# A product of experts with the tokens standing still: 512 moving columns instead of 288, and the sample rows apart in column groups

## The chip, the cores and the metric

The kernel runs on one NeuronCore of a Trainium2 chip, as one launch. The core has five engines that run their own instruction streams and meet only at semaphores: TensorE (PE, matrix products), VectorE (DVE), ScalarE (ACT), GpSimd (POOL) and SyncE (SP, here the queue that issues most transfers). The metric is device time in microseconds; 1143.01 is the median of three runs of the kernel before.

## The reference, cut to what matters

One layer of a decoder: a projection, a pooling mixer, a sparse attention, an output projection, and then a retrieval over 128 x 128 one-neuron experts (PEER). There are 256 prompt tokens and 32 sample tokens, 288 in all, of width 1024. Only the last part and its residual are touched:

```python
def trunk_layer(x, ...):
    ...
    x = x + jnp.concatenate([ya, yb], axis=-1) @ w_o
    x = x + peer(rms_norm(x, norm2_g), w_pq, sub_keys, expert_u, expert_v)

def peer(h, w_pq, sub_keys, expert_u, expert_v):
    ...
    # per token: top 16 of each of two lists of 128 keys, top 16 of their 256 sums, 8 heads:
    # eidx (N, 128) expert numbers, g (N, 128) softmax weights
    def body(args):
        xt, et, gt = args
        a = jax.nn.gelu(jnp.einsum('td,ted->te', xt, expert_u[et]), approximate=False)
        return jnp.einsum('te,ted->td', gt * a, expert_v[et])
```

The prompt rows and the sample rows are separate outputs. In the setup N_EXPERTS is 16384, D_MODEL 1024, PEER_HEADS 8.

## The kernel before, in words

The retrieval is computed densely. The experts are cut into NU = 128 blocks of 128 experts. In the **U stage** block n's inner products with all 288 tokens are made (`prod_u`), gelu is applied, and they are multiplied with the gate, which is zero for experts that a token did not choose. The result lies in `store`, 128 experts on the partitions, blocks by tokens along the row. In the **V stage** (`prod_v`) block v's gated activations are multiplied with its 128 x 1024 piece of expert_v and summed over all 128 blocks in PSUM.

Both products are made in the format fp32r with a correction: an operand is split into a high part and the rest (`w_hi`, `w_lo` of the weights, `h_hi`, `h_lo` of the tokens, `ag_hi`, `ag_lo` of the gated activations), and three terms are summed, high by high, high by low, low by high. ScalarE makes the high parts (`split_w`, `high_ag`; both through the helper `copy`, line 962), GpSimd subtracts to get `w_lo` (`low_w`, line 1340), VectorE subtracts to get `ag_lo` (`low_ag`, line 1655). SyncE loads each block's 512 KB into a ring of four (`w_raw`), and a slot is loaded again when PE has done the block (`prod_done`).

In the V stage before, the weights stand still: for each of eight chunks c of 128 output features there are three matmuls with the weights as the stationary operand (128 x 128) and all 288 tokens moving, into one PSUM bank for each chunk. The output is transposed, features on the partitions, and so is the residual `x_res`.

What comes ahead of it: VectorE selects the sample tokens' 256 best keys out of 1028 by rounds of `max` and `match_replace` on `work_s`, and line 1486 turns the result into a mask; PE spreads it (`sample_spread`, line 754) and goes on with the routing's query product (`rq`, line 729, and `rs`, line 744), the sample softmax follows (`pnew_ready` marks its two halves), then the sample's output projection (line 791), which uses four groups of 32 array columns side by side (`tile_position=(0, 32 * j)`), and the first weights of the U stage. During blocks 0 to 12 of the U stage PE also makes the sample tokens' query products (`rq_s`, line 849, in column groups too), and VectorE does the routing's top-16 selection until it has the slots, for which PE waits ahead of block 36 (transposes, line 477). From block 44 on the gates are spread (line 889) in 72 steps.

Each engine's order is the order in which its function below issues; nothing is reordered by a planner. `FRONT` is the number of U blocks that are written out, the others are loops. `tr` is the transpose on PE, line 477. The profile gives a matmul's line, and for fp32 operands it has two records for one matmul of the code.

## Time and profile before

| | us |
|---|---|
| median of three runs | 1143.01 (1140.9 to 1143.41) |
| the profiled execution | 1139.06 |
| its span, first to last instruction | 1136.9 |
| mean granted TensorE clock | 0.995 |
| PE busy / share | 1113.7 / 98% |
| GpSimd busy / share | 706.6 / 62% |
| VectorE busy / share | 616.2 / 54% |
| ScalarE busy / share | 430.9 / 38% |

A matmul's busy time is counted until its last result has left the array, and matmuls overlap, so a PE that is busy all the time says little about its pace. For that one reads the distance from one start to the next in a timeline.

### The profile page before, as it was taken

What the parts mean: (1) busy time and instruction counts of PE and PEld (TensorE: products, weight loads), DVE (VectorE), ACT (ScalarE), POOL (GpSimd) and SP (SyncE); (2) the same over time, 40 slices, a digit from 0 to 9 for tenths busy, and PEclk for the clock granted to TensorE, in tenths of its full rate; (3) what the DMA queues carried; (4) which work ended last, traced back from release to release, by engine and by line L of the source; (5) the groups of instructions that cost most, each with busy time, mean ns of one, the idle gap of its engine ahead of it and who ended that gap; (6) DMA issues with size and microseconds to landing.
All of it is one profiled execution on the core that took longest, in us unless ns stands there. A gap on an engine that the chain in (4) does not pass through costs nothing.

```text
span 1136.9 us, 24346 instructions
## 1 busy us (share of the span) xinstructions
PE 1113.7 (98%) x8263; PEld 1045.3 (92%) x8263; DVE 616.2 (54%) x1327; ACT 430.9 (38%) x750; POOL 706.6 (62%) x406
## 2 busy tenths in 40 slices
PE   7999998999999999999999999999999999999998
PEld 3448887899999999999999999999999999999998
DVE  2659999299998166666666671332222322222332
ACT  2133231343454433333333334444444444444442
POOL 4643434065776755555555557777777777777775
PEclk9999999999999999999999999999999999999999
DMA  9444577177654544444444445445555545444554
GB/s 334 121 115 130 169 260 265 66 274 256 206 160 137 167 130 129 126 128 126 127 127 128 128 128 160 154 166 166 166 166 166 165 162 165 161 166 161 164 166 174
DMA packets 64503, 186.62 MB, mean 164 GB/s; under 512 B 9157, under 2 KB 21069, under 8 KB 64068
## 3 DMA queue, kind: packets, MB, share of 16 engines
q1 hardware_dynamic: 59356, 178.60, 48.6%
q0 software_dynamic: 3824, 6.97, 2.0%
q10 hardware_dynamic: 1280, 0.53, 0.2%
q8 instruction: 22, 0.36, 0.1%
q14 instruction: 21, 0.17, 0.0%
HBM read 183.23 MB, written 3.00 MB: 164 GB/s over the span
## 4 chain that ended last, share of the span: by engine, by line
PE 78%; DVE 20%; DMA 1%; ACT 1%; issue 1%; DVEq 0%; SPq 0%
PE psum L944 36%; PE psum L878 25%; PE psum L889 6%; PE psum L493 4%; DVE top L1411 3%; DVE work_s L1412 2%; DVE rwork L1529 1%; DVE cand L1547 1%; PE psum L702 1%; PE psum L729 1%; DVE hit L1576 1%; DVE picked L1579 1%; DVE slots L1582 1%; DVE si L1535 1%; DVE si L1528 1%; PE psum L509 1%
## 5 line engine op out<-in xcount | busy, mean ns | idle before, releaser
L1340 POOL TENSOR_TENSOR w_lo<-w_raw,w_hi 128x1024 fp32r<-128x1024 f32 x256 | 614.5, 2402 | 316.3 <-ACT w_hi L962 316.3
L962 ACT ACTIVATE w_hi<-w_raw 128x1024 fp32r<-128x1024 f32 x256 | 271.7, 1061 | 238.4 <-DMA w_raw<-expert_v 224.7
L878 PE MATMUL psum<-h_hi,w_hi 128*128 128x288 f32 x1024 | 310.1, 303 | 0.0
L944 PE MATMUL psum<-ag_hi,w_hi 128*128 128x288 f32 x1024 | 301.4, 294 | 1.3 <-DVE ag_lo L1655 1.3
L878 PE MATMUL psum<-h_lo,w_hi 128*128 128x288 f32 x1024 | 302.6, 295 | 0.0
L878 PE MATMUL psum<-h_hi,w_lo 128*128 128x288 f32 x1024 | 302.1, 295 | 0.0
L944 PE MATMUL psum<-ag_hi,w_lo 128*128 128x288 f32 x1024 | 301.8, 295 | 0.0
L944 PE MATMUL psum<-ag_lo,w_hi 128*128 128x288 f32 x1024 | 301.5, 294 | 0.0
L1655 DVE TENSOR_TENSOR ag_lo<-store,ag_hi 128x288 fp32r<-128x288 f32 x128 | 121.1, 946 | 284.1 <-PE psum L944 282.9
L878 PEld LDWEIGHTS psum<-h_hi,w_hi 128*128 128x128 f32 x1024 | 192.8, 188 | 1.6 <-issue 1.6
L944 PEld LDWEIGHTS psum<-ag_hi,w_hi 128*128 128x128 f32 x1024 | 192.0, 188 | 1.5 <-issue 1.5
L878 PEld LDWEIGHTS psum<-h_hi,w_lo 128*128 128x128 f32 x1024 | 193.2, 189 | 0.0
L878 PEld LDWEIGHTS psum<-h_lo,w_hi 128*128 128x128 f32 x1024 | 193.1, 189 | 0.0
L944 PEld LDWEIGHTS psum<-ag_hi,w_lo 128*128 128x128 f32 x1024 | 192.1, 188 | 0.0
L944 PEld LDWEIGHTS psum<-ag_lo,w_hi 128*128 128x128 f32 x1024 | 192.0, 188 | 0.0
L1183 ACT ACTIVATE psum<-psum 128x288 f32<-128x288 f32 (+36 forms) x84 | 24.7, 294 | 211.3 <-PE psum L878 211.3
L1634 DVE COPY store<-psum 128x336 f32<-128x336 f32 (+35 forms) x72 | 25.9, 360 | 121.3 <-PE psum L889 121.3
L889 PE MATMUL psum<-i_hot,j_hot 128*128 128x128 f32 x576 | 75.8, 275 | 0.0
L889 PEld LDWEIGHTS psum<-i_hot,j_hot 128*128 128x128 f32 x576 | 71.4, 191 | 0.0
L340 POOL DMA_DIRECT2D v_cache<-cache_v x64 | 34.2, 534 | 56.9 <-issue 52.1
L729 PE MATMUL psum<-h,w_slice 128*128 128x256 f32 x256 | 60.1, 388 | 0.1
L729 PEld LDWEIGHTS psum<-h,w_slice 128*128 128x128 f32 x256 | 48.2, 194 | 7.5 <-issue 1.4
(261 smaller groups left out, 1058.4 us busy)
## 6 DMA issues: line engine op xcount, KB each, us to landing
w_raw<-expert_ut SPq DMA_DIRECT2D x128, 512.0 KB, 3.6
w_raw<-expert_v SPq DMA_DIRECT2D x128, 512.0 KB, 3.3
w_slice<-w_pq_cols SPq DMA_DIRECT2D x32, 512.0 KB, 5.6
w_most<-w_in_blocks SPq DMA_DIRECT2D x8, 699.0 KB, 12.8
w_slice<-w_o_half SPq DMA_DIRECT2D x8, 512.0 KB, 4.2
v_cache<-cache_v POOLq DMA_DIRECT2D x64, 64.0 KB, 3.3
w_o_sb<-w_o_half SPq DMA_DIRECT2D x8, 512.0 KB, 8.0
kT<-cache_kt SPq DMA_DIRECT2D x44, 64.0 KB, 2.0
```

The costliest lines, as they stand in the source:

```text
L340: eng.dma_start(dst[:, bass.ds((4 * i + (first + u)) * width, width)], cache[0, bass.ds(pg[u], 1), :, :].rearrange("a p d -> (a p) d")).th ...
L493: return pe.matmul(psum[:, 4 + (i + 1) % 4, 0:ZQ], hT[:, k, t * P:(t + 1) * P], w_cols(j, k), start=(k == 0), stop=(k == KC - 1))
L729: mm = pe.matmul(psum[:, r % 2, 0:SEQ], w_slice[:, (KC + r) % SLICES, k, :], h2[:, k, 0:SEQ], start=(k == 0), stop=(k == KC - 1))
L878: mm = pe.matmul(psum[:, 2 + s, 0:NT], a[:, s, c, :], b[:, c, :], start=(i == 0), stop=(i == 3 * KC - 1))
L889: mm = pe.matmul(psum[:, 6 + s % 2, b * NU:(b + 1) * NU], j_hot[:, s % 2, b, :], i_hot[:, s % 2, b, :], start=True, stop=True, skip_group_ ...
L944: mm = pe.matmul(psum[:, (c + 6) % 8, 0:NT], a[:, s, c, :], b, start=(first and i == 0), stop=(last and i == 2), skip_group_check=True)
L962: return act.activation(out, in_, ACT.Copy)
L1183: a = act.activation(psum[:, 2 + s, 0:done], psum[:, 2 + s, 0:done], ACT.Gelu)
L1340: pool.tensor_tensor(w_lo[:, s], w_raw[:, s], w_hi[:, s].bitcast(F32), ALU.subtract).then_inc(S["w_lo_ready"], 1)
L1411: settle(dve.max(best, left))
L1634: dve.tensor_copy(part[:, n:NU], g[:, n:NU])
L1655: dve.tensor_tensor(ag_lo[:, s % 2, :], store[:, bass.ds(v, 1)].rearrange("p a t -> p (a t)"), ag_hi[:, s, :].bitcast(F32), ALU.subtract). ...
```

## The change

Five things are changed.

1. In the V stage the operands change places. The gated activations of 128 prompt tokens are stationary, and 512 columns of expert_v move. There are four outputs of 128 tokens x 512 features (`Y_ORDER`), three terms each: 12 matmuls for a block. First come the eight with `w_hi`, then, behind the wait for `w_lo_ready`, the four with `w_lo_v`.
2. The 32 sample tokens are kept out of that. Their gated activations (`ag_s`, copied by VectorE) are stationary in plain fp32, and `w_raw` moves: four matmuls of 256 columns, one in each group of 32 array columns, ahead of the twelve.
3. The residual is kept by token. During U blocks 13, 15, 17, 19 and 21 PE transposes x1 (`x1_rows`), ScalarE copies it to `x_rows`, and SP saves it at block 23 instead of saving `xT` at block 11. `FRONT` goes from 16 to 24 for that. The final addition and the output are by rows.
4. GpSimd's low part of the weights goes to a buffer of two (`w_lo_v`) in the V stage, where it was a ring of four; it waits for `prod_done`.
5. GpSimd's `h_lo` of the prompt tokens waits for `pnew_ready`, 2 as well.

```diff
-    ag_hi = at("ag_hi", cur[0], [P, RING, NT], F32R)
-    ag_lo = at("ag_lo", cur[0] + RING * NT, [P, 2, NT], F32R)
+    ag_hi = at("ag_hi", cur[0], [P, RING, SEQ], F32R)
+    ag_lo = at("ag_lo", cur[0] + RING * SEQ, [P, 2, SEQ], F32R)
+    ag_s = at("ag_s", cur[0] + (RING + 2) * SEQ, [P, 2, NS])
...
+    w_lo_v = at("w_lo_v", cur[0], [P, 2, KC, P], F32R)
...
-    FRONT = 16
+    FRONT = 24
+    X_ROWS_AT = (13, 15, 17, 19, 21)
+    Y_ORDER = ((0, 0), (0, 1), (1, 0), (1, 1))
...
+            def x1_rows(i):
+
+                if i >= 2:
+                    pe.wait_ge(S["x_rows_copied"], i - 1)
+                for q in range(4):
+                    if i < 4:
+                        mm = tr(psum[:, 6 + i % 2, q * P:(q + 1) * P], xT[:, 4 * (i % 2) + q, (i // 2) * P:(i // 2 + 1) * P])
+                        continue
+                    for a in range(2):
+                        mm = pe.matmul(psum[32 * q:32 * q + 32, 6, a * P:(a + 1) * P], xT[:, 2 * q + a, SEQ:NT],
+                                       ident[:, :], start=True, stop=True, tile_position=(0, 32 * q),
+                                       skip_group_check=True)
+                mm.then_inc(S["x_rows_psum"], 1)
...
             def prod_v(s, v, first=False, last=False):
 
                 pe.wait_ge(S["w_hi_ready"], v + (NU + 1))
-                pe.wait_ge(S["w_lo_ready"], v + (NU + 1))
                 pe.wait_ge(S["ag_hi_ready"], v + 1)
                 pe.wait_ge(S["ag_lo_ready"], v + 1)
-                for c in range(KC):
-                    if first and c == 0:
-                        pe.wait_ge(S["g_done"], G_STEPS)
-                    if first and c >= 4:
-                        pe.wait_ge(S["act_free"], NU + (c - 7))
-                    i = 0
-                    for a, b in ((w_hi, ag_hi[:, s, :]), (w_hi, ag_lo[:, s % 2, :]), (w_lo, ag_hi[:, s, :])):
-                        mm = pe.matmul(psum[:, (c + 6) % 8, 0:NT], a[:, s, c, :], b, start=(first and i == 0), stop=(last and i == 2), skip_group_check=True)
-                        i += 1
+                if first:
+                    pe.wait_ge(S["g_done"], G_STEPS)
+                    pe.wait_ge(S["act_free"], NU - 3)
+                for j in range(4):
+                    mm = pe.matmul(psum[32 * j:32 * j + 32, 2, 0:2 * P], ag_s[:, s % 2, :],
+                                   w_raw[:, s, 2 * j:2 * j + 2, :].rearrange("p c d -> p (c d)"), start=first,
+                                   stop=last, tile_position=(0, 32 * j), skip_group_check=True)
+                if last:
+                    mm.then_inc(S["y_psum"], 1)
+                def v_term(i, a, b, start=False, stop=False):
+
+                    t, h = Y_ORDER[i]
+                    return pe.matmul(psum[:, (i + 6) % 8, :], a[:, t * P:(t + 1) * P],
+                                     b[:, 4 * h:4 * h + 4, :].rearrange("p c d -> p (c d)"), start=start, stop=stop,
+                                     skip_group_check=True)
+
+                for i in range(4):
+                    v_term(i, ag_hi[:, s, :], w_hi[:, s], start=first)
+                    v_term(i, ag_lo[:, s % 2, :], w_hi[:, s])
+                pe.wait_ge(S["w_lo_ready"], v + (NU + 1))
+                for i in range(4):
+                    mm = v_term(i, ag_hi[:, s, :], w_lo_v[:, s % 2], stop=last)
                     if last:
                         mm.then_inc(S["y_psum"], 1)
...
             pool.wait_ge(S["h_hi_p"], 1)
+            pool.wait_ge(S["pnew_ready"], 2)
             pool.tensor_tensor(h_lo[:, :, 0:SEQ], h2[:, :, 0:SEQ], h_hi[:, :, 0:SEQ].bitcast(F32), ALU.subtract
                                ).then_inc(S["h_lo_p"], 1)
...
-            with pool.Fori(1, LAST // RING) as m:
+            with pool.Fori(1, NU // RING) as m:
                 for s in range(RING):
                     low_w(s, RING * m + s)
+
+            def low_v(s, v, done):
+                pool.wait_ge(S["w_hi_ready"], v + (NU + 1))
+                pool.wait_ge(S["prod_done"], done)
+                pool.tensor_tensor(w_lo_v[:, s % 2], w_raw[:, s], w_hi[:, s].bitcast(F32), ALU.subtract
+                                   ).then_inc(S["w_lo_ready"], 1)
+
+            for s in range(RING):
+                low_v(s, s, NU + max(s - 1, 0))
+            with pool.Fori(1, NU // RING) as m:
+                for s in range(RING):
+                    low_v(s, RING * m + s, RING * m + (NU + s - 1))
...
-                dve.tensor_tensor(ag_lo[:, s % 2, :],
-                                  store[:, bass.ds(v, 1)].rearrange("p a t -> p (a t)"),
-                                  ag_hi[:, s, :].bitcast(F32), ALU.subtract).then_inc(S["ag_lo_ready"], 1)
+                row = store[:, bass.ds(v, 1)].rearrange("p a t -> p (a t)")
+                dve.tensor_copy(ag_s[:, s % 2, :], row[:, SEQ:NT])
+                dve.tensor_tensor(ag_lo[:, s % 2, :], row[:, 0:SEQ], ag_hi[:, s, :].bitcast(F32), ALU.subtract
+                                  ).then_inc(S["ag_lo_ready"], 1)
...
-            for c in range(KC):
-                dve.wait_ge(S["y_psum"], c + 1)
-                dve.tensor_tensor(x_res[:, c, :], x_res[:, c, :], psum[:, (c + 6) % 8, 0:NT], ALU.add
-                                  ).then_inc(S["y_added"], 1)
+            dve.wait_ge(S["x_res_in"], 32)
+            dve.wait_ge(S["y_psum"], 1)
+            dve.tensor_tensor(x_res_s[:, :], x_res_s[:, :], psum[:, 2, 0:2 * P], ALU.add).then_inc(S["y_added"], 1)
+            for i, (t, h) in enumerate(Y_ORDER):
+                dve.wait_ge(S["y_psum"], i + 2)
+                rows = x_res[:, t, BANK * h:BANK * (h + 1)]
+                dve.tensor_tensor(rows, rows, psum[:, (i + 6) % 8, :], ALU.add).then_inc(S["y_added"], 1)
```

On PE, one block inside the V stage's loop stood so before; the last three rows go on in the same pattern up to 24 matmuls:

```order
L944 MATMUL psum<-ag_hi,w_hi 128x288 [waits ag_lo_ready,ag_hi_ready]
L944 MATMUL psum<-ag_lo,w_hi 128x288
L944 MATMUL psum<-ag_hi,w_lo 128x288
L944 MATMUL psum<-ag_hi,w_hi 128x288
L944 MATMUL psum<-ag_lo,w_hi 128x288
L944 MATMUL psum<-ag_hi,w_lo 128x288
```

And the same block on PE now, whole:

```order
L965 REGISTER_ALU [waits w_hi_ready]
L971 MATMUL psum<-w_raw,ag_s 32x256 [waits ag_lo_ready,ag_hi_ready]
L971 MATMUL psum<-w_raw,ag_s 32x256 x3
L979 MATMUL psum<-w_hi,ag_hi 128x512
L979 MATMUL psum<-w_hi,ag_lo 128x512
L979 MATMUL psum<-w_hi,ag_hi 128x512
L979 MATMUL psum<-w_hi,ag_lo 128x512
L979 MATMUL psum<-w_hi,ag_hi 128x512
L979 MATMUL psum<-w_hi,ag_lo 128x512
L979 MATMUL psum<-w_hi,ag_hi 128x512
L979 MATMUL psum<-w_hi,ag_lo 128x512
L979 MATMUL psum<-w_lo_v,ag_hi 128x512 [waits w_lo_ready]
```

Three more of the last row follow. The wait for the low weights has moved behind eight matmuls, and four matmuls on 32 array columns stand at the head of each block.

On GpSimd the U stage's and the V stage's subtractions were one loop, before:

```order
L1335 TENSOR_TENSOR h_lo<-h_90,h_hi 128x8x256 [waits h_hi_p]
L1340 TENSOR_TENSOR w_lo<-w_raw,w_hi 128x1024 [waits w_hi_ready]
L1345 TENSOR_TENSOR h_lo<-h_90,h_hi 128x8x32 [waits h_hi_s]
L1340 TENSOR_TENSOR w_lo<-w_raw,w_hi 128x1024 [waits w_hi_ready] x3
L1350 UNCONDITIONAL_BRANCH
```

Now, on GpSimd, the first of them has a further wait, and the V stage has rows of its own:

```order
L1387 TENSOR_TENSOR h_lo<-h_92,h_hi 128x8x256 [waits pnew_ready,h_hi_p]
L1392 TENSOR_TENSOR w_lo<-w_raw,w_hi 128x1024 [waits w_hi_ready]
L1397 TENSOR_TENSOR h_lo<-h_92,h_hi 128x8x32 [waits h_hi_s]
...
L1409 TENSOR_TENSOR w_lo_v<-w_raw,w_hi 128x1024 [waits prod_done,w_hi_ready] x4
L1414 UNCONDITIONAL_BRANCH
```

What moved: the first row now stands behind VectorE's sample softmax, and the V stage's subtractions behind PE's blocks.

## Rows read from the trace of the kernel before

**Rows 1.** The page: busy times, and the group of one line.

```profile
PE 1113.7 (98%) x8263; PEld 1045.3 (92%) x8263; DVE 616.2 (54%) x1327; ACT 430.9 (38%) x750; POOL 706.6 (62%) x406
...
L1340 POOL TENSOR_TENSOR w_lo<-w_raw,w_hi 128x1024 fp32r<-128x1024 f32 x256 | 614.5, 2402 | 316.3 <-ACT w_hi L962 316.3
```

**Rows 2.** The chain that ended last, by line, and its V part in time.

```profile
PE psum L944 36%; PE psum L878 25%; PE psum L889 6%; PE psum L493 4%; DVE top L1411 3%; DVE work_s L1412 2%; DVE rwork L1529 1%; DVE cand L1547 1%; PE psum L702 1%; PE psum L729 1%; DVE hit L1576 1%; DVE picked L1579 1%; DVE slots L1582 1%; DVE si L1535 1%; DVE si L1528 1%; PE psum L509 1%
...
725.34 404.50 PE psum L944 x3051
```

**Rows 3.** Busy time in a stretch of V: length, PE, PEld, DVE, ACT, POOL, clock, DMA.

```profile
900.00:1000.00 100.00, 100.00 (x757) 100.00 (x756) 28.99 (x32) 43.67 (x63) 75.47 (x32) 1.00 0.50 163
```

**Rows 4.** PE's timeline, 187 to 224 us: start, length, what.

```profile
187.79 0.61 PE L744 MATMUL psum<-keysT,q_ring 128*128 128x128 f32 x4
188.23 3.62 PE L729 MATMUL psum<-h,w_slice 128*128 128x256 f32 x16
191.69 0.61 PE L744 MATMUL psum<-keysT,q_ring 128*128 128x128 f32 x4
...
218.79 3.66 PE L791 MATMUL psum<-w_o_sb,catT 128*32 128x256 f32 x64
222.38 1.13 PE L729 MATMUL psum<-h,w_slice 128*128 128x256 f32 x4
223.34 0.38 PE L477 MATMUL psum<-ident,wo_rows 128*128 128x128 f32 x2
```

**Rows 5.** PE's timeline around the first L849 group.

```profile
238.43 0.29 PE L878 MATMUL psum<-h_hi,w_lo 128*128 128x288 f32 x1
238.65 1.95 PE L849 MATMUL psum<-w_slice,h 128*32 128x128 f32 x64
240.54 0.40 PE L878 MATMUL psum<-h_hi,w_hi 128*128 128x288 f32 x1
240.78 0.30 PE L878 MATMUL psum<-h_lo,w_hi 128*128 128x288 f32 x1
```

**Rows 6.** PE's timeline behind 363 us, and a stretch: length, busy, clock, DMA.

```profile
363.89 0.82 PE L477 MATMUL psum<-ident,slots 128*32 128x128 f32 x3 [2.29 <-DVE slots L1600]
364.75 0.44 PE L878 MATMUL psum<-h_lo,w_hi 128*128 128x288 f32 x1
364.99 0.44 PE L878 MATMUL psum<-h_hi,w_lo 128*128 128x288 f32 x1
...
364.40:368.00 3.60, 3.60 (x20) 0.63 0.00 0
```

**Rows 7.** Timelines of POOL, DVE and PE, 189 to 224 us, and one stretch.

```profile
189.76 4.53 POOL L1335 TENSOR_TENSOR h_lo<-h,h_hi 128x2048 fp32r<-128x2048 f32 x1
...
190.64 4.74 DVE L1486 TENSOR_TENSOR work_s<-work_s,score_s 32x1028 f32<-32x1028 f32 x1
197.17 1.22 DVE L1493 TENSOR_TENSOR log_s<-log_s,psum 128x1024 f32<-128x1024 f32 x1 [1.01 <-PE psum L754]
223.76 0.48 DVE L1510 TENSOR_TENSOR xT<-xT,psum 128x128 f32<-128x128 f32 x2 [15.39 <-PE psum L477]
...
196.22 0.91 PE L754 MATMUL psum<-bias_s,fold 32*128 32x512 bf16 x3 [3.93 <-DVE bias_s L1488]
197.06 5.06 PE L729 MATMUL psum<-h,w_slice 128*128 128x256 f32 x16
...
195.00:215.00 20.00, 18.78 (x208) 0.91 0.08 27
```

**Rows 8.** The start of V on PE; durations (min/median/max ns) of L1655.

```profile
725.34 0.37 PE L944 MATMUL psum<-ag_hi,w_hi 128*128 128x288 f32 x1 [1.30 <-DVE ag_lo L1655]
...
L1655 DVE TENSOR_TENSOR ag_lo<-store,ag_hi x128: 457/926/2424, 722.7 to 1126.4; 128x288 fp32r<-128x288 f32 x128
```

**Rows 9.** The end of V: DVE's additions, and PE's last matmul.

```profile
1129.93 3.18 DVE L1672 TENSOR_TENSOR x_res<-x_res,psum 128x288 f32<-128x288 f32 x8 [2.55 <-PE psum L944]
...
1132.33 0.29 PE L944 MATMUL psum<-ag_hi,w_lo 128*128 128x288 f32 x1
```

More of the change, by code:

```diff
@@ L289, in hybrid_kernel @@
     eq_ps = psum[:, 1, :].rearrange("p (b i) -> p b i", b=NB)
-    x1_save = nc.dram_tensor("x1_save", [P, KC, NT], F32, kind="Internal").ap()
+    x1_save = nc.dram_tensor("x1_save", [P, 2, D], F32, kind="Internal").ap()
+    x1_save_s = nc.dram_tensor("x1_save_s", [P, 2 * P], F32, kind="Internal").ap()
     S = Named(nc, ctx)
@@ L455, in _ @@
                         load_slice(q + i)
[L456 to L457 removed]
+                if n == FRONT - 1:
+                    sp.wait_ge(S["x_rows_copied"], len(X_ROWS_AT))
+                    sp.dma_start(x1_save, x_rows[:]).then_inc(S["x1_saved"], 16)
+                    sp.dma_start(x1_save_s, x_rows_s[:]).then_inc(S["x1_saved"], 16)
             with sp.Fori(FRONT // RING + 1, NU // RING) as m:
@@ L466, in _ @@
             sp.dma_start(x_res[:], x1_save).then_inc(S["x_res_in"], 16)
-            for c in range(0, KC, 2):
-                sp.wait_ge(S["y_added"], c + 2)
-                sp.dma_start(y_t[:, c:c + 2, :], x_res[:, c:c + 2, :]).then_inc(S["out_done"], 16)
-            sp.wait_ge(S["out_done"], 16 * (1 + KC // 2))
+            sp.dma_start(x_res_s[:], x1_save_s).then_inc(S["x_res_in"], 16)
+            sp.wait_ge(S["y_added"], 1)
+            sp.dma_start(y_rows_s, x_res_s[:]).then_inc(S["out_done"], 16)
+            for i, (t, h) in enumerate(Y_ORDER):
+                sp.wait_ge(S["y_added"], i + 2)
+                sp.dma_start(y_rows[:, t, BANK * h:BANK * (h + 1)], x_res[:, t, BANK * h:BANK * (h + 1)]
+                             ).then_inc(S["out_done"], 16)
+            sp.wait_ge(S["out_done"], 16 * (2 + len(Y_ORDER)))
         @block.tensor
@@ L904, in _ @@
                     rs_s(n // 3 - 1)
+                if n in X_ROWS_AT:
+                    x1_rows(X_ROWS_AT.index(n))
             with pe.Fori(FRONT // RING, SLOTS_AT // RING) as m:
@@ L1202, in _ @@
                     copy(q_tr[:, i % 2, :], psum[:, 7, 0:P]).then_inc(S["q_tr_copied"], 1)
+                if n in X_ROWS_AT:
+                    i = X_ROWS_AT.index(n)
+                    act.wait_ge(S["x_rows_psum"], i + 1)
+                    if i < 4:
+                        a = copy(x_rows[:, i // 2, BANK * (i % 2):BANK * (i % 2 + 1)], psum[:, 6 + i % 2, :])
+                    else:
+                        a = copy(x_rows_s[:, :], psum[:, 6, 0:2 * P])
+                    a.then_inc(S["x_rows_copied"], 1)
                 if n == 13:
@@ L1241, in high_ag @@
                     act.wait_ge(S["prod_done"], v + (NU - 3))
-                copy(ag_hi[:, s, :], store[:, bass.ds(v, 1)].rearrange("p a t -> p (a t)")
+                copy(ag_hi[:, s, :], store[:, bass.ds(v, 1)].rearrange("p a t -> p (a t)")[:, 0:SEQ]
                      ).then_inc(S["ag_hi_ready"], 1)
@@ L1728 @@
     r = run_bass_kernel_spmd(nc, [a], core_ids=[0])
-    y = np.ascontiguousarray(r.results[0]["y_t"].transpose(2, 1, 0)).reshape(SEQ + DB * DS, D)
-    return (y[:SEQ].reshape(1, SEQ, D), y[SEQ:].reshape(DB, DS, D)) + tuple(r.results[0][n] for n, _ in outs[1:])
+    y = np.ascontiguousarray(r.results[0]["y_rows"].transpose(1, 0, 2)).reshape(1, SEQ, D)
+    y_s = np.ascontiguousarray(r.results[0]["y_rows_s"].reshape(4, DB * DS, 2 * P).transpose(1, 0, 2))
+    return (y, y_s.reshape(DB, DS, D)) + tuple(r.results[0][n] for n, _ in outs[2:])
```

16 lines of the change are left out of this document (9 added, 7 removed).

## The prediction

> **What bounds the kernel now.** I read the page first, then the chain that ended last, the busy time by stretches, PE's timeline at the places where it changes its kind of work, and the waits. On the page TensorE (PE) is busy for 98% of the span, GpSimd (POOL) for 62%, VectorE (DVE) for 54% [rows 1]; but busy PE is not PE at its peak, so the chain is the better witness: 25% of it is one line of PE, L878, the U stage, and 36% is another, L944, the V stage [rows 2]. In that stage nothing stops PE: from 725.34 us the chain has 3051 matmul records in 404.50 us, 132.6 ns each, without a wait [rows 2], so a block of 24 matmuls takes 24 x 132.6 = 3.182 us. GpSimd works 75.5 us in 100 us there, VectorE 29 and ScalarE 44 [rows 3]. The V stage therefore costs what PE's instruction stream costs, and that is where this change has to be priced. Ahead of the U stage, up to 232 us, the chain runs through VectorE's selection and short PE pieces, and a microsecond saved there counts in full.
>
> **The V stage, per block.** The change takes 24 matmuls of 288 columns away and puts in 12 of 512 columns (four outputs, three terms) and four fp32 matmuls of 256 columns, one for each group of 32 array columns.
>
> The four small ones have an exact likeness: L791 issues the same shape, fp32, stationary 32 tokens, 256 columns, j innermost. It gave 64 records for 32 matmuls, so an fp32 matmul is two records. A plain fp32 stretch of 256 columns has 16 records in 191.69 - 188.23 = 3.46 us, a step of 0.216 [rows 4]. L791's 64 records go in 16 steps of four, so the four groups do run side by side: 16 x 0.216 = 3.456. Two steps a block: 0.432 us. But L791 lasts 222.38 - 218.79 = 3.59 us, 0.13 more than its steps, and the four L729 records behind it take 0.96 (to 223.34) against 4 x 0.216 = 0.864, 0.10 more [rows 4]. The whole trip, out of fp32r matmuls and back into them, stands at L849, inside the U stage: 0.22 from the last 288-column matmul where 0.133 is usual, 1.89 for 16 steps that take 0.110 elsewhere (187.79 to 188.23 for four), 0.24 to the second matmul behind it: 0.09 + 0.13 + 0.11 = 0.33 [rows 4, 5]. I take 0.334. Before, that trip was made in a few places; now it is made in each of 128 blocks.
>
> The Trainium skill weighs in here from both sides. "TensorEngine Tiling (Array Packing)", Key Properties, says that changing the tiling mode drains the engine; it has no price for it. "TensorE: Matmul & The Clock Gate", Measured speedup vs the span model, has a group of column tiles last one matmul plus about 4 ns for each further tile, and no charge around it; by that the sample part would be the 0.432 alone and the block 0.33 us shorter than I sum it.
>
> The 12 wide ones have no likeness: no fp32r matmul here has another width than 288. Bare streaming of 288 columns is 0.120 us at 2.4 GHz (at 1.2 GHz, granted clock 0.5 to 0.63, the step is 0.24, 364.75 to 364.99 [rows 6]); the full-clock step is 0.1326, so 12.6 ns come on top. The fp32 steps have only some 3 ns on top (0.216 for two passes of 256 columns). Three readings for 512 columns: the 12.6 are paid once per matmul, 213.3 + 12.6 = 226; they grow with the columns, 132.6 x 512/288 = 236; or they vanish when a matmul is long, as with fp32, 216. I take 226, the middle one: the one row there is says 12.6 per matmul, and nothing in it says per column. 216 and 236 are the bounds.
>
> Block: 12 x 0.226 + 0.432 + 0.334 = 3.478 us (3.358 with 216, 3.598 with 236), against 3.182. Over 128 blocks: **+37.9 us** (+22.5, +53.2). Even with free overheads per matmul the trip of 0.33 outweighs what longer matmuls give back: 24 x 12.6 = 0.30 us was all the excess there was.
>
> What else moves there is covered. GpSimd's subtraction (2.40 us [rows 1]) now waits until the block two before is done, but PE asks for it only behind eight wide matmuls, about 2.6 us into the block; GpSimd has a block and a half. ScalarE copies 256 instead of 288 columns, 44% busy. The DMA per block is the same 512 KB in a longer period.
>
> **The front.** The row part of h_lo (POOL L1335, 4.53 us) moves behind the sample softmax. Before, it ran from 189.76 to 194.29, and VectorE's L1486, 1028 elements of 32 rows, took 4.74 us beside it; a two-source operation of 128x1024 takes 1.22 alone (L1493) [rows 7]. VectorE lost 3.5 us, and PE stood 3.93 us for its result. After that wait PE ran at a lower pace: the 16 records of L729 behind it took 5.06 instead of 3.62, 1.44 more, with the granted clock at 0.91 over the stretch 195 to 215 [rows 4, 7], and the L754 group ahead of them shares in it; I count 1.6 that a wait of 0.4 would not cost. In the new place GpSimd has VectorE's idle time: VectorE stands 15.39 us before L1510 [rows 7]. Everything up to the first product hangs on this chain: **-5.1 us** (-3.5 if the slow stretch stays).
>
> **The U stage.** New on PE: 16 transposes and a group of eight small fp32 matmuls. No transpose stands in the rows; I price one at the step of a 128-column record, 0.11 [rows 4], 16 x 0.11 = 1.8. The last group (eight matmuls, 16 records) has 16 steps of 0.11 if pairs on one column group run one behind the other and 4 if all run side by side, plus one trip: 0.8 to 2.1, I take 1.3. Together 3.1. Against that stands PE's only wait of the U stage, 2.29 us at 363.89 for the routing's slots, with a slow stretch behind it: 20 matmul records in 3.6 us at clock 0.63 where 27 fit, and half-pace pieces before, some 1.2 us [rows 6]. PE now comes 3.1 us later to a result that doesn't move, so both go: 3.1 - 2.3 - 1.2 = **-0.4 us** (-0.9 to +0.4). The five copies lie in idle time of ScalarE (38% busy over the span [rows 1]); the save to memory is as large as before and waits at a place where only later loads are queued behind it on SP, with three blocks already loaded.
>
> **Start and end of V.** Before, PE waited 1.30 us at 725.34 for VectorE's ag_lo, which then took 2.42 us, its longest, where its median is 0.93 [rows 8], GpSimd's subtractions running beside it. GpSimd now starts on V only when the last product is done, and PE needs fewer of the gates: 1.3 us go. But GpSimd then runs two subtractions on end while VectorE wants ag_lo for the second block; I give 0.5 back: **-0.8 us** (-1.5 to +0.7). At the end VectorE added each output while PE made the next: eight in 3.18 us, the last 0.78 us behind the last matmul's start [rows 9]. Now the four wide ones stop within 0.7 us, and four additions of 512 columns, 0.6 us each (between 0.40 for 288 and 1.22 for 1024 [rows 7, 9]), end 2.2 us behind it: **+1.4 us**. The output's transfer is of about the same size.
>
> **Sum.** -5.1 - 0.4 - 0.8 + 37.9 + 1.4 = +33.0. On the profiled execution (span 1136.9, with what lies around it 1139.06) that makes 1172.1. The median of the runs is 1143.01, 3.95 above that execution; the time asked for is compared with such medians, so I add the change to it: **1176.0 us**.
>
> **Rivals.**
> - *The excess per matmul vanishes with width* (step 216): 1176.0 - 15.4 = 1160.6. For it: the fp32 steps of 128 and of 256 columns carry 3 ns at most, whatever their length. Against it: their loads come at most once in 107 ns of streaming too (0.110 for 128 columns), and there the excess is as small, so a load alone doesn't make it; something of fp32r does. Chance 0.17. The Trainium skill, "TensorE: Matmul & The Clock Gate", Back-to-back issue gap, gives this as its rule (columns / 2.4 + 2.5 ns when warm); for 288 columns it would say 122.5 where the trace has 132.6, so here it is off for fp32r.
> - *It grows with the columns* (236): 1176.0 + 15.3 = 1191.3. For it: at half clock there is no excess at all, as if full speed outran the operand's supply. Against it: nothing in the trace. Chance 0.28.
> - *The trip is not paid in the loop* (small matmuls slip in beside the wide ones). Block 12 x 0.226 + 0.432 = 3.144, -4.9 us over 128, in all 1143.0 - 5.1 - 0.4 - 0.8 - 4.9 + 1.4 = 1133.2, faster. It decides from a trip below 0.08 us on (0.20 with 216). Against it: both places that are read above, 0.33 each. For it: those were single trips in other surroundings. Chance 0.06.
> - *VectorE becomes the bound.* Its copy and subtraction for block v wake with GpSimd's subtraction, both by the end of block v-2. Between the two, GpSimd can step in: 0.2 + 2.40 + 0.42 and some 0.1 of signals make 3.1 us; there are 3.48 less about 0.25, 3.2. With GpSimd at 2.5 or more it binds, and each 0.1 us costs 12.8. ag_lo went up to 2424 ns in this stage [rows 8]. At 0.1 us: 1189. Chance 0.07.
> - Forecast: 0.42.
>
> **How the numbers follow.** Forecast and the two neighbours of the step and VectorE's case hold 0.94 of the chance; the range goes from 1158 (216, less 2.6 for the small terms) to 1193 (236, plus 1.7). Faster by over 0.2% only in the third rival, 0.06; within 0.2% (2.3 us, about what a measurement here can tell) 0.02; slower 0.92.
>
> **What would show it.** In the V stage of the changed kernel: a period of 3.48 us from one block's first small matmul to the next; steps of 0.226 between wide matmuls; about 0.33 us at the seams, where the first wide matmul's record is longer than its fellows. L1486's heir at 1.2 us with PE waiting under 1 us, and no 2.3 us wait before the slots' transposes. It would be wrong if the seams were invisible, if PE waited for ag_lo each block, or if the wide step were outside 216 to 236.

## The result and the profile after

The change makes the kernel slower: 1177.09 us in the median of 4 runs (1175.0 to 1177.97) against 1142.23 us (1140.9 to 1143.41) for the kernel before on the same chip, a ratio of 1.0303 [1.0283, 1.0323]. The prediction was 1176.0 us, in a range from 1158 to 1193. The profiled execution of the changed kernel took 1177.8 us, with a span of 1176.1.

The page's first part again, and from its fifth part VectorE's costliest group (line, engine, operation, out<-in, count | busy us, mean ns of one | idle time before it and what ended it), to set against [rows 1]:

```profile
PE 1157.4 (98%) x7783; PEld 938.0 (80%) x7783; DVE 833.0 (71%) x1452; ACT 428.5 (36%) x755; POOL 707.5 (60%) x406
...
L1720 DVE COPY ag_s<-store 128x32 f32 (+1 forms) x128 | 300.3, 2346 | 104.8 <-PE psum L979 103.1
```

TensorE is 98% busy as before, with fewer and longer matmuls. VectorE is up from 54% to 71%, and one line makes it: a copy of 32 columns, 2346 ns on average.

The stretch that answers to [rows 3] (length, busy time of PE, PEld, DVE, ACT and POOL, then clock, DMA share, GB/s):

```profile
900.00:1000.00 100.00, 100.00 (x573) 66.39 (x566) 77.83 (x57) 39.48 (x58) 68.67 (x29) 1.00 0.46 148
```

PE is busy without a gap; GpSimd has 29 subtractions in it instead of 32: fewer blocks come through in the same time.

PE's timeline in V, one whole block from seam to seam (start, length to the end of the last, line, what, how many):

```profile
899.62 0.64 PE L971 MATMUL psum<-w_raw,ag_s 128*32 128x256 f32 x8
900.19 0.50 PE L979 MATMUL psum<-w_hi,ag_hi 128*128 128x512 f32 x1
900.53 0.39 PE L979 MATMUL psum<-w_hi,ag_lo 128*128 128x512 f32 x1
...
902.14 1.07 PE L979 MATMUL psum<-w_lo_v,ag_hi 128*128 128x512 f32 x4
903.14 0.64 PE L971 MATMUL psum<-w_raw,ag_s 128*32 128x256 f32 x8
```

The period is 903.14 - 899.62 = 3.52 us; 124 of the stage's 127 periods have it. Read it by starts. From the second wide matmul (900.53) to the ninth (902.14) are seven steps in 1.61 us, 0.230 each; of the four of w_lo_v the 1.07 us less one record's 0.39 are three steps, 0.227. Over the block the wide step is 0.2294. What is left of 3.520 after 12 x 0.2294 = 2.753 and two small steps of 0.216 is the trip, the loss at going from the wide matmuls into the column groups and back: 0.335 us. It shows where it was expected: the first wide matmul behind the small ones is 0.50 long instead of 0.39, and the next starts 0.34 behind it (900.19 to 900.53) instead of 0.23.

The front and the borders of the stages, on PE, VectorE and GpSimd, against [rows 6 to 9]:

```profile
192.30 1.22 DVE L1550 TENSOR_TENSOR work_s<-work_s,score_s 32x1028 f32<-32x1028 f32 x1
194.36 0.60 PE L768 MATMUL psum<-bias_s,fold 32*128 32x512 bf16 x3 [0.42 <-DVE bias_s L1552]
194.89 3.72 PE L743 MATMUL psum<-h,w_slice 128*128 128x256 f32 x16
205.02 4.54 POOL L1387 TENSOR_TENSOR h_lo<-h,h_hi 128x2048 fp32r<-128x2048 f32 x1 [14.93 <-DVE pnew L1568]
228.58 0.38 PE L892 MATMUL psum<-h_hi,w_hi 128*128 128x288 f32 x1
...
360.97 0.50 PE L491 MATMUL psum<-ident,slots 128*32 128x128 f32 x3 [0.35 <-DVE slots L1664]
...
719.56 0.29 PE L892 MATMUL psum<-h_hi,w_lo 128*128 128x288 f32 x1
719.78 0.64 PE L971 MATMUL psum<-w_raw,ag_s 128*32 128x256 f32 x8
...
1170.09 2.48 DVE L1740 TENSOR_TENSOR x_res<-x_res,psum 128x512 f32<-128x512 f32 x4 [1.75 <-PE psum L979]
```

VectorE's operation takes 1.22 us instead of 4.74, PE waits 0.42 us instead of 3.93, and the 16 records behind the wait take 3.72 us instead of 5.06. The waits of 2.29 and 1.30 us at the slots and at the start of V have become 0.35 and none. Yet the first product (228.58) is only 3.5 us earlier than before (232.08), and VectorE's operation starts 1.7 us later than its forerunner did (190.64). From the start of that operation to the first product it is 36.28 us against 41.44, 5.2 us less; the rest was lost ahead of it. A row of before and the windows of the two executions say where (before first, then after; the last three figures are clock, DMA share, GB/s):

```profile
232.08 0.38 PE L878 MATMUL psum<-h_hi,w_hi 128*128 128x288 f32 x1
...
110.00:148.00 38.00, 36.15 (x205) 30.30 (x207) 35.54 (x49) 9.36 (x21) 14.96 (x28) 1.00 0.61 192
```

```profile
110.00:148.00 38.00, 36.13 (x181) 31.21 (x183) 33.92 (x48) 9.37 (x21) 15.04 (x28) 0.96 0.59 179
```

In this execution of the changed kernel TensorE had a stretch at the lower clock level between 110 and 148 us, in code that the change doesn't touch. Of the eight kernels below that keep its front, none has it there. In six of them the first product stands at 226.5 to 227.0 us, 5.1 us or more earlier than before; the other two come as late as the changed kernel, with a granted clock of 0.94 over their first 60 us.

### The profile page after: what moved, and what is told of

The parts are those of the page before. It is cut to its first block, busy times and chain, and to the rows that moved or that the text cites. A ratio compares the mean times of both kernels' runs of the same rounds, so it can differ in the third digit from the quotient of the medians.

```text
span 1176.1 us, 23563 instructions
## 1 busy us (share of the span) xinstructions
PE 1157.4 (98%) x7783; PEld 938.0 (80%) x7783; DVE 833.0 (71%) x1452; ACT 428.5 (36%) x755; POOL 707.5 (60%) x406
## 4 chain that ended last, share of the span: by engine, by line
PE 87%; DVE 9%; DMA 2%; SPq 1%; issue 1%; ACT 0%; DVEq 0%; ACTq 0%
PE psum L892 33%; PE psum L979 32%; PE psum L971 6%; PE psum L903 5%; PE psum L507 3%; DVE top L1475 2%; DVE work_s L1476 2%; DMA w_rest<-w_in_blocks 2%; PE psum L743 2%; PE psum L716 1%; PE psum L491 1%; PE psum L686 1%; PE psum L863 1%; SPq L374 1%; DVE work_p L1476 1%; DVE picked L1643 1%
## 5 line engine op out<-in xcount | busy, mean ns | idle before, releaser
L1392 POOL TENSOR_TENSOR w_lo<-w_raw,w_hi 128x1024 fp32r<-128x1024 f32 x128 | 307.4, 2404 | 195.6 <-ACT w_hi L1005 195.5
L1409 POOL TENSOR_TENSOR w_lo_v<-w_raw,w_hi 128x1024 fp32r<-128x1024 f32 x128 | 308.1, 2408 | 143.6 <-PE psum L979 138.2
L1720 DVE COPY ag_s<-store 128x32 f32 (+1 forms) x128 | 300.3, 2346 | 104.8 <-PE psum L979 103.1
L979 PE MATMUL psum<-w_hi,ag_hi 128*128 128x512 f32 x512 | 214.3, 419 | 0.0
L979 PE MATMUL psum<-w_hi,ag_lo 128*128 128x512 f32 x512 | 201.5, 394 | 0.0
L979 PEld LDWEIGHTS psum<-w_hi,ag_hi 128*128 128x128 f32 x512 | 96.0, 187 | 69.0 <-issue 52.7
L979 PE MATMUL psum<-w_lo_v,ag_hi 128*128 128x512 f32 x512 | 136.8, 389 | 0.0
L979 PEld LDWEIGHTS psum<-w_lo_v,ag_hi 128*128 128x128 f32 x512 | 96.1, 188 | 20.9 <-POOL w_lo_v L1409 0.4
L979 PEld LDWEIGHTS psum<-w_hi,ag_lo 128*128 128x128 f32 x512 | 96.4, 188 | 17.2
L971 PE MATMUL psum<-w_raw,ag_s 128*32 128x256 f32 x1024 | 81.8, 391 | 0.0
```

The source lines that it names most:

```text
L971: mm = pe.matmul(psum[32 * j:32 * j + 32, 2, 0:2 * P], ag_s[:, s % 2, :], w_raw[:, s, 2 * j:2 * j + 2, :].rearrange("p c d -> p (c d)"), s ...
L979: return pe.matmul(psum[:, (i + 6) % 8, :], a[:, t * P:(t + 1) * P], b[:, 4 * h:4 * h + 4, :].rearrange("p c d -> p (c d)"), start=start, ...
L1392: pool.tensor_tensor(w_lo[:, s], w_raw[:, s], w_hi[:, s].bitcast(F32), ALU.subtract).then_inc(S["w_lo_ready"], 1)
L1409: pool.tensor_tensor(w_lo_v[:, s % 2], w_raw[:, s], w_hi[:, s].bitcast(F32), ALU.subtract).then_inc(S["w_lo_ready"], 1)
L1720: dve.tensor_copy(ag_s[:, s % 2, :], row[:, SEQ:NT])
```

## The experiments

Each kernel is the changed kernel with one edit, but for the one with the copy out of the way, which builds on the one ahead of it, and the last, which is the kernel before with one edit. "Before" in each comparison ran on the same chip. Distances to the changed kernel are distances between separate series of runs, on three chips or more: the kernel before has medians from 1140.12 to 1142.23 us in these series, so up to 2 us of such a distance can be the chip's or that of the executions taken.

**Late h_lo taken back.** GpSimd no longer waits before the row part of h_lo:

```diff
-            pool.wait_ge(S["pnew_ready"], 2)
             pool.tensor_tensor(h_lo[:, :, 0:SEQ], h2[:, :, 0:SEQ], h_hi[:, :, 0:SEQ].bitcast(F32), ALU.subtract
```

> The changed kernel with GpSimd's row part of h_lo back where it was, ahead of the sample softmax. Theory: VectorE's comparison of 1028 elements again takes 4.7 us instead of 1.2, PE waits 3.9 us for it and runs on at the lower clock for a while: 5.2 us more than the changed kernel, about 1182. Rival: only VectorE's 3.5 us come back and the slower stretch of PE was chance: about 1180.5. Second rival: the wait moved is worth nothing because the v_cache pages or the softmax are late anyway: 1177.

Measured: 1182.43 us (1182.05 to 1182.82), ratio 1.0368 [1.0341, 1.0394], 5.3 us above the changed kernel. Its VectorE, GpSimd and PE:

```profile
190.37 4.74 DVE L1549 TENSOR_TENSOR work_s<-work_s,score_s 32x1028 f32<-32x1028 f32 x1
...
189.50 4.52 POOL L1386 TENSOR_TENSOR h_lo<-h,h_hi 128x2048 fp32r<-128x2048 f32 x1
...
195.96 1.03 PE L768 MATMUL psum<-bias_s,fold 32*128 32x512 bf16 x3 [3.94 <-DVE bias_s L1551]
196.92 6.33 PE L743 MATMUL psum<-h,w_slice 128*128 128x256 f32 x15
```

The whole of the old picture is back: VectorE's operation at 4.74 us beside GpSimd's, the wait of 3.94 us, and slow matmuls behind it. From the start of VectorE's operation to the first product (233.43) it is 43.06 us, where the changed kernel has 36.28. The front's gain is this one wait.

**Wide matmuls cut in two.** Each 512-column matmul becomes two of 256; same stationary operand, twice the instructions:

```diff
-                    return pe.matmul(psum[:, (i + 6) % 8, :], a[:, t * P:(t + 1) * P],
+                    for k in range(2):
+                        mm = pe.matmul(psum[:, (i + 6) % 8, 2 * P * k:2 * P * (k + 1)], a[:, t * P:(t + 1) * P],
```

> The changed kernel with each of the 12 wide matmuls cut into two of 256 columns, same operands. It measures what a full-width fp32r matmul costs beside its columns (0.2294 us for 512 columns, 0.1326 for 288). If the extra is fixed per matmul (13 to 16 ns): step 0.120 to 0.123, block 3.65 to 3.71 us, 17 to 24 us more, 1194 to 1201. If it grows with the columns: step 0.115, block 3.52, 1177. If a stationary load with what goes with it takes 0.132 whatever the width (288 columns would then have been bound by the load): step 0.132, block 3.94, 54 us more, about 1231.

Measured: 1190.62 us (1189.79 to 1191.92), ratio 1.0442 [1.0414, 1.047]; the period is 3.63 us. That is nearest to the first case, and a little below its ranges (3.65 to 3.71, 1194 to 1201). Its timeline:

```profile
900.43 0.40 PE L980 MATMUL psum<-w_hi,ag_lo 128*128 128x256 f32 x2
900.67 0.40 PE L980 MATMUL psum<-w_hi,ag_hi 128*128 128x256 f32 x2
```

Two matmuls of 256 columns take 0.24 us (0.120 each by the records' starts), 13 ns above bare streaming (106.7). For 288 columns it was 12.6 above 120, for 512 it is 13 to 16 above 213.3. So the excess is nearly one price per matmul: neither proportional to the columns (that would give 0.118 x 2 = 0.236 for 512, where 0.2294 was measured) nor absent in long ones. At 256 columns "per matmul" and "per column" lie close (0.119 and 0.118); it is 256, 288 and 512 together that tell them apart.

**Order of the terms.** Four matmuls with ag_hi, then four with ag_lo, instead of in turn:

```diff
                 for i in range(4):
                     v_term(i, ag_hi[:, s, :], w_hi[:, s], start=first)
+                for i in range(4):
                     v_term(i, ag_lo[:, s % 2, :], w_hi[:, s])
```

> The changed kernel with the eight matmuls on w_hi in another order: four with ag_hi, then four with ag_lo, where they alternated. In the changed kernel the eight steps on w_hi are 0.228 to 0.236 us and the four on w_lo_v 0.227. If alternating stationary operands are what costs the difference: all steps 0.227, 2 to 4 us less, 1173 to 1175. If it is the moving operand's place in memory or other engines' traffic: no difference, 1177.

Measured: 1177.14 us (1175.86 to 1179.04), ratio 1.0323 [1.0293, 1.0352], and a period of 3.52 us. The order is worth nothing.

**The trip once for two blocks, first attempt.** The small matmuls of an even block wait and run with those of the odd one; the even block's w_raw is held a block longer for them:

```diff
-                    sp.wait_ge(S["prod_done"], RING * m + (NU + s - RING + 1))
+                    sp.wait_ge(S["prod_done"], RING * m + (NU + s - RING + 1 + (s + 1) % 2))
...
+                if s % 2:
+                    pe.wait_ge(S["ag_s_ready"], v + 1)
+                    for b in (s - 1, s):
+                        for j in range(4):
```

> The changed kernel with the small matmuls of two blocks made together at the head of every second block, the same matmuls in number and kind. Theory (the trip into the column groups and back costs 0.335 us each time): 64 trips fewer, a pair of blocks takes 6.705 instead of 7.040 us, 21.4 us less, about 1155.5. Rival (the loss lies in the small matmuls' own columns or in the wide steps, whatever surrounds them): 1177. Second rival (VectorE's chain of copy and subtraction binds once the blocks are unequal): between, 1160 to 1170, with PE waiting for ag_lo or ag_s.

Measured: 1202.64 us (1200.42 to 1203.64), ratio 1.054 [1.051, 1.057]; missed by 47 us, to the wrong side. The costliest of its waits from 800 to 1000 us (who waits for whom: us in total, times, longest):

```profile
ACT w_hi L1009 <- DMA w_raw<-expert_v: 129.7, 29, 8.9
```

Two heads of pairs on PE:

```profile
877.36 1.07 PE L972 MATMUL psum<-w_raw,ag_s 128*32 128x256 f32 x16
...
884.07 1.07 PE L972 MATMUL psum<-w_raw,ag_s 128*32 128x256 f32 x16
```

ScalarE waits up to 8.9 us for the weights: holding a slot of the ring of four longer sends two loads off together and late, and everything behind them is late. The edit carried a second change, and that one decided the time. The trace still says something on the trip: where the loads are in time, a pair of blocks takes 884.07 - 877.36 = 6.71 us, the 6.705 that the theory has for one trip in two blocks.

**The trip once for two blocks, one block early.** Ahead of an even block's wide matmuls stand its own small ones and the next block's, so that every slot is released as before; VectorE copies the sample columns of both blocks at once, ahead of the even block's ag_lo:

```diff
+                if s % 2 == 0:
+                    pe.wait_ge(S["w_hi_ready"], v + (NU + 2))
+                    for b in (s, s + 1):
+                        for j in range(4):
...
+                if s % 2 == 0:
+                    dve.tensor_copy(ag_s[:, s:s + 2, :],
+                                    store[:, bass.ds(v, 2)][:, :, SEQ:NT])
```

> The small matmuls of two blocks stand together again, this time one block early: ahead of the even block's wide matmuls those of this block and of the next one, so no slot of the weight ring is held longer than in the changed kernel. If the 0.335 us that each block loses goes at the change between the small column-group matmuls and the wide ones (theory), two blocks lose it once: 2 x (12 x 0.2294 + 0.432) + 0.335 = 6.705 us instead of 7.040, 64 x 0.335 = 21.4 us less than the changed kernel, 1155.7 us, between 1153 and 1158. If the time is lost anew at each group of four small matmuls, whatever stands ahead of it (rival), 1177 us as now. If the copy of the samples' activations, two blocks' at once, comes late behind GpSimd's subtraction (second rival), waits on it appear in the chain and the time lies in between.

Measured: 1182.41 us (1181.47 to 1184.14), ratio 1.0374 [1.0353, 1.0395]; a miss, in the direction of the second rival and beyond it. One turn of the chain:

```profile
903.94 3.36 DMA w_raw<-expert_v
...
908.37 0.41 ACT ag_hi L1009
...
908.85 1.83 issue
910.68 0.42 DVE ag_lo L1727
...
911.33 1.07 PE psum L974 x16
```

The 1.83 us that the chain calls issue is the copy: VectorE's timeline has it from 908.32 for 2.44 us, with GpSimd's subtraction beginning at 908.31. A weight block is now wanted one block earlier, and load, ScalarE's two operations, the copy and ag_lo make a loop that takes longer than PE's work.

**The same, with the copy out of the way.** The copy for the next two blocks is made behind the odd block's ag_lo:

```diff
+                if s % 2 and not last:
+                    copy_ag_s((s + 1) % RING, v + 1)
```

> The pair of blocks again, with VectorE's copy of the samples' activations taken out of the way: it is made for the next two blocks after the odd block's ag_lo, instead of ahead of the even block's. In the pair kernel before this one VectorE's copy could start only 2.4 us before TensorE wanted ag_lo, and the block took 3.58 us on a loop over the weight load, the two engines' copies and TensorE. If that copy was what closed the loop (theory), TensorE bounds again and the trip is paid once for two blocks: 1155.7 us, between 1153 and 1158. If the loop over the load is closed by something else, since a weight block is wanted one block earlier than in the changed kernel (rival), it stays at 1170 to 1182 us with waits on w_hi or ag_lo in the chain.

Measured: 1166.16 us (1165.24 to 1166.74), ratio 1.0223 [1.0197, 1.025]: 10.9 us below the changed kernel and 10.5 above what the theory gave, so outside its range and outside the rival's. The chain, nearly all PE now:

```profile
895.67 2.62 DVE ag_lo L1724
...
898.52 1.07 PE psum L974 x16
899.59 5.66 PE psum L983 x24
...
909.39 2.63 DVE ag_lo L1724
```

The heads of three pairs in PE's timeline:

```profile
898.52 1.07 PE L974 MATMUL psum<-w_raw,ag_s 128*32 128x256 f32 x16 [0.27 <-DVE ag_lo L1724]
...
905.18 1.07 PE L974 MATMUL psum<-w_raw,ag_s 128*32 128x256 f32 x16
...
912.24 0.64 PE L974 MATMUL psum<-w_raw,ag_s 128*32 128x256 f32 x8 [0.28 <-DVE ag_lo L1724]
```

From 898.52 to 905.18 two blocks go by in 6.66 us, with 16 small records and one trip, where two blocks of the changed kernel take 7.04; 6.705 had been worked out, with every wide step at 0.2294, and here those of the second block are 0.227. So the trip is paid for each change to the column groups, not for each group of four. The next pair takes 7.06, and so it goes on: 32 of 63 pairs take 6.66 to 6.71 us, the other 31 take 7.04 to 7.09. What is missing of the 21.4 us is mostly a new wait: every second time ag_lo itself (0.41 us alone) lasts 2.62 us beside GpSimd's subtraction, and PE stands for it (6.1 us in 22 times from 800 to 1100 us, so 0.28 each). That is once in four blocks, 9 us over 128.

**One column group of the four.** The loop over the groups ends after the first:

```diff
-                for j in range(4):
+                for j in range(1):
```

> Of the four small matmuls of a block only that of the first column group is left, so three quarters of the sample rows of y are left out. The four ran beside each other in 0.432 us. If the round trip is paid for going into any 32-column group (theory), the block stays at 12 x 0.2294 + 0.432 + 0.335 = 3.520 us and the time at 1177 us. If the trip is the wait for four groups to drain (rival), it shrinks towards a quarter of 0.335 us, and the time towards 1145 us. The fp32 matmul over all 128 columns took the place of the four at 0.06 us more than nothing for the trip, so this tells the group itself from the number of groups.

Measured: 1173.06 us (1172.87 to 1173.7), ratio 1.0288 [1.0262, 1.0314]. Its timeline:

```profile
903.24 0.62 PE L971 MATMUL psum<-w_raw,ag_s 128*32 128x256 f32 x2
903.78 0.50 PE L979 MATMUL psum<-w_hi,ag_hi 128*128 128x512 f32 x1
...
906.74 0.62 PE L971 MATMUL psum<-w_raw,ag_s 128*32 128x256 f32 x2
```

The period is 3.50 us: the other three groups cost 0.02 together, the trip stands as it was. The number of groups is not what it costs. The time is 4 us below the 1177 expected. Of the spans' distance 2.6 us are these 0.02 in each block, and 2.0 lie ahead of the first product (226.55 against 228.58).

**Full width in place of the groups.** One fp32 matmul with 128 stationary columns takes the place of the four:

```diff
-                for j in range(4):
-                    mm = pe.matmul(psum[32 * j:32 * j + 32, 2, 0:2 * P], ag_s[:, s % 2, :],
+                mm = pe.matmul(psum[:, 2, 0:2 * P], w_raw[:, s, 4, :],
```

> In each block one full-width fp32 matmul (128 stationary columns, 256 moving) takes the place of the four in 32-column groups; it multiplies a block of the weights with itself, so the sample rows of y are left out. By the theory that the round trip is the price of using column groups, it vanishes: 12 x 0.2294 + 0.432 = 3.185 us for a block instead of 3.520, 1177.1 - 128 x 0.335 = 1134.2 us. By the rival that it is the price of going from fp32r to fp32 operands and back, the block stays at 3.52 us and the time at 1177 us. If both share it, between them.

Measured: 1139.54 us (1138.92 to 1141.16), ratio 0.9994 [0.9983, 1.0005], 37.6 us below the changed kernel, between what the theory (1134.2) and the rival (1177) gave and near the theory. Its timeline:

```profile
900.11 0.63 PE L970 MATMUL psum<-w_raw 128*128 128x256 f32 x2
900.40 0.58 PE L978 MATMUL psum<-w_hi,ag_hi 128*128 128x512 f32 x1
...
903.34 0.61 PE L970 MATMUL psum<-w_raw 128*128 128x256 f32 x2
```

900.11 to 903.34 is a period of 3.23 us (3.24 on average over the stage). Less 12 wide steps (at 0.2294, as in the changed kernel) and two small ones, 0.05 is left of the trip. So going from fp32r to fp32 and back costs some 0.05 us, going into 32-column groups and back the other 0.28. The Trainium skill, "TensorEngine Tiling (Array Packing)", Key Properties, says that a change of the tiling mode drains the engine. This run and the one with a single group agree that the change costs something whatever the number of groups, and put its price at 0.28 us for the way in and back.

**No small matmuls** in any block but the first and the last:

```diff
-                for j in range(4):
+                for j in range(4 if first or last else 0):
```

> The small matmuls are left out of all blocks but the first and the last, so the sample rows of y miss most of their sum; everything else stays. By the theory the wide matmuls alone take 12 x 0.2294 = 2.753 us for a block; TensorE then no longer bounds the loop everywhere, since VectorE's pair (the copy of 2.35 us behind GpSimd's subtraction, and 0.41 us) and the waits between the engines take about 2.99 us for a block. So 1177.1 - 126 x 0.53 = 1110 us, with waits of TensorE on what VectorE hands over; if TensorE stays the bound (rival), 1177.1 - 126 x 0.767 = 1080 us; a wide step that needs more time than 0.2294 without the small ones between would show as a block over 2.753 us without a wait.

Measured: 1109.14 us (1107.76 to 1110.26), ratio 0.9725 [0.9706, 0.9744]. The number is that of the theory, its loop only in part. The chain through four blocks:

```profile
903.74 5.77 PE psum L979 x24
...
909.67 3.17 DMA w_raw<-expert_v
...
913.90 0.41 ACT ag_hi L1005
...
914.38 0.84 issue
915.22 0.42 DVE ag_lo L1721
...
915.78 0.47 PE psum L979
```

Two blocks of PE, then load, ScalarE, VectorE (the copy hides in the 0.84 called issue), and PE again: 915.78 - 903.74 = 12.04 us for four blocks, 3.01 each. VectorE is on the loop, but so is the load. The changed kernel has 14.08 us for the same four blocks, which is why none of this binds there.

**The kernel before with the late h_lo alone.** The one edit of the change that gained:

```diff
             pool.wait_ge(S["h_hi_p"], 1)
+            pool.wait_ge(S["pnew_ready"], 2)
```

> The kernel before with one edit of the change alone: GpSimd's subtraction that makes h_lo of the prompt tokens waits for the new pool rows, as in the changed kernel, so that it no longer stands in the way of VectorE there. By the theory the front's gain of the change is this wait and nothing else, and taking it back cost the changed kernel 5.3 us; so 1142.2 - 5.2 = 1137.0 us, faster than both kernels, between 1136 and 1138.5. By the rival that the gain of the front belongs to the new placing of buffers or of the program in memory, 1142 us.

Measured: 1135.43 us (1133.72 to 1135.93, 6 runs) against 1140.12 (17 runs), ratio 0.9955 [0.9939, 0.997]. It is 4.7 us faster than the kernel before, the fastest kernel of this study that computes everything, and 0.6 us below the range expected. Its profiled execution:

```profile
194.47 0.60 PE L754 MATMUL psum<-bias_s,fold 32*128 32x512 bf16 x3 [0.41 <-DVE bias_s L1489]
195.01 3.72 PE L729 MATMUL psum<-h,w_slice 128*128 128x256 f32 x16
...
360.49 0.50 PE L477 MATMUL psum<-ident,slots 128*32 128x128 f32 x3 [2.29 <-DVE slots L1601]
```

The front is as in the changed kernel, with 36.28 us from the start of VectorE's operation to the first product, and the wait of 2.29 us at the slots is still there.

## Why the prediction was right

Its terms were made against the profiled execution, so the spans are compared: 1176.1 - 1136.9 = +39.2 us, where the terms added up to +33.0.

- **The V stage**, forecast +37.9, measured from first to last matmul 1170.3 - 719.8 = 450.6 against 407.0: +43.6 us. The mechanism held in all its parts: a period without a wait, small matmuls in two steps of 0.216, a trip of 0.335 (0.334 forecast). That the trip belongs to the change into column groups, and is paid for each such change, was argued from two places; the pair of blocks at 6.66 us, the single group and the full-width matmul show it. The one mis-sized term is the wide step, 0.2294 instead of 0.226: 12 x 128 x 0.0034 = 5.2 us. Another 0.3 us lies in the stage's first two periods, 3.81 and 3.56 us: in the first, PE's first matmul on the low weights starts at 722.46, right behind the subtraction that GpSimd had begun at 720.00.
- **The readings of the wide step.** Of 216, 226 and 236 the middle one was nearest, and the 256-column kernel shows it as a price per matmul of some 13 ns; at 512 columns it is 14 on w_lo_v and mostly 18 to 20 on w_hi, 16 in the mean, so "per matmul" is the nearest of the three readings and not exact. The Trainium skill's rule of columns / 2.4 + 2.5 ns ("TensorE: Matmul & The Clock Gate", Back-to-back issue gap), which the page gives for the isolated gap of one matmul and which was the rival with 216, gives 109, 122.5 and 215.8 ns for 256, 288 and 512 columns where the traces have 120, 132.6 and 229: for fp32r the measurement decides against it. The price per matmul doesn't explain why the steps on w_hi take 0.231 and those on w_lo_v 0.227. The order of the terms isn't it, and in the kernel with paired blocks and the copy out of the way some blocks ran all 12 at 0.227. Which other engine's traffic or which sequence makes the 4 ns was not found.
- **The front**, forecast -5.1, in the profiled execution -3.5. The part on VectorE and PE came as forecast (PE's wait 0.42, full pace behind it), and 1.7 us were lost to a slow stretch elsewhere that comes and goes between executions. Counted from the start of VectorE's operation, behind that stretch, the front is 41.44 us before and 36.28 after, -5.16. The single-edit kernels give it as 5.3 us one way and 4.7 the other in the medians; their profiled executions had slow stretches of their own (0.97 and 0.94 over the first 60 us), and behind them 43.06 and 36.28 us.
- **The U stage**, forecast -0.4: from the first to the last product 490.98 us against 491.66, -0.7. PE's new work took the place of the wait for the slots, and the slow stretch behind that wait is gone.
- **The start of V**, forecast -0.8: 0.22 us from the last product to the first small matmul against 1.60, -1.4; the half microsecond set aside for the second block's ag_lo was not needed, since it was made by 722.78 and PE came to that block at 723.59.
- **The tail**, forecast +1.4: 1.2 us. VectorE's four additions take 2.48 us.
- **The step from span to median.** The prediction added the change to the median of the runs, on the ground that the profiled execution of before was 3.95 us below it. The medians moved by 34.9 us, the profiled executions by 38.7: that of before was a fast one of its kind, that of after was not. The forecast for the profiled execution was 1172.1, 5.7 us under the 1177.8 that it took; the 3.95 us added, and 0.7 by which the median of after lies below its profiled execution, took 4.7 of these back. That the total is 1.1 us off is luck to this extent. The base was a lucky one too: the median of three runs, 1143.01, lies above the medians of the longer series of the same kernel beside the experiments, 1140.12 to 1140.82.
- **The rivals.** The trip is paid in the loop. VectorE is not the bound: it works 78 us in 100, and its copy takes 2.37 us in each block, but PE never waits for it in the steady stage. This rival had the mechanism nearly right: the two operations do stand behind GpSimd's subtraction, but that one starts first and the copy lasts as long as it does, instead of GpSimd stepping in between the two. In the three kernels with paired blocks and in the one without small matmuls (3.01 us for a block) PE did wait for ag_lo; with the full-width matmul, at 3.24, it did not in the steady stage.

## What to carry to other kernels

A few small matmuls in 32-column groups are cheap in themselves, and the way into the groups and back is not: price it per change, from a place in the same program where it is made once, and put small work together or issue it at full width if the loop is short. Add up all the parts of a block ahead of such a change. Here the wide matmuls stream 0.32 us less (12 x 512 columns instead of 24 x 288 at 2.4 GHz) and carry 0.11 us less in prices per matmul (12 x 16.1 ns instead of 24 x 12.6), and the small ones cost 0.43: these three are nearly even, so the 0.34 us by which a block got longer is the trip. The full-width kernel shows it from the other side, with 3.24 us for a block against 3.18 before. And when work is moved between blocks, look at which buffer is held longer or wanted earlier: of three attempts to save the trip two lost more than they saved and the third lost half of it, to the ring of four and to VectorE behind GpSimd, neither of which had anything to do with TensorE.

## What the hardware showed beyond that

- A copy of 128x32 fp32 elements on VectorE took 2.35 to 2.44 us in 122 of 122 cases of the steady stage (730 to 1160 us), always started beside GpSimd's two-source subtraction of 2.40 us; the shortest in the stage took 0.181:

```profile
903.37 2.37 DVE L1720 COPY ag_s<-store 128x32 f32 x1 [0.83 <-PE psum L979]
...
905.65 0.41 DVE L1721 TENSOR_TENSOR ag_lo<-store,ag_hi 128x256 fp32r<-128x256 f32 x1
...
903.29 2.40 POOL L1409 TENSOR_TENSOR w_lo_v<-w_raw,w_hi 128x1024 fp32r<-128x1024 f32 x1 [1.12 <-PE psum L979]
```

  The copy begins 0.08 us behind the subtraction and ends with it, and the subtraction that follows it on VectorE runs at its own pace. Such a row's length is GpSimd's, not its own. The Trainium skill, "SBUF — State Buffer", SBUF: two separate sides, has GpSimd and a VectorE instruction with two SBUF inputs or in a 2-port mode exclude each other on a shared pair of ports for the whole of an instruction; the rows agree for the copy and, in the kernel with the paired blocks, for ag_lo at 2.62 us.
- Four fp32 matmuls in four column groups took 0.02 us more than one of them alone (period 3.52 against 3.50).
- TensorE idle for 3.9 us (early h_lo) had 15 records in 6.33 us behind it, granted clock 0.83 over 195 to 215 us; idle for 0.42 us it had 16 in 3.72 at clock 1.00. The wait costs more than its length.
- Slow stretches of TensorE's clock in the first 150 us come and go between executions whose code is the same up to there (granted clock 0.96 over 110 to 148 us in one and 1.00 in the others; 0.94, 0.97 or 1.00 over the first 60 us), and move everything behind them by up to 2 us. An edit worth less than that needs several runs, not one trace.
